# Out-projections of three mixers: the first weight units multiplied with tokens 0 to 127 ahead of the rest

## What is computed

```python
x = x + even_mixer(h, ...)     # ends in  concat(attention, delta rule) @ even_w_out
...
x = x + odd_mixer(h, ...)      # ends in  attention @ odd_w_out
...
m = gate_a * y_a + gate_b * y_b + gate_c * y_c
x = x + m @ w_out
```

## Time and profile before

| what | value |
|---|---|
| median of 3 runs | 1814.69 us (1814.22 to 1814.96) |
| profiled execution | 1815.65 us |
| its span, first to last instruction | 1813.9 us |
| TensorE busy with products (PE) | 1720.6 us, 95% |
| VectorE, ScalarE busy | 1296.1 us (71%), 992.0 us (55%) |
| mean granted TensorE clock | 0.976 |

### The profile page before, as it was taken

One profiled execution on the slowest core, in us unless ns is written; L12 is line 12 of the kernel. 1 busy time (PEld: TensorE's weight loads), 2 busy tenths in 40 slices (PEclk: granted clock), 3 DMA queues, 4 the chain that ended last, 5 costly groups with the idle time before them and its releaser, 6 DMA issues.

```text
span 1813.9 us, 38431 instructions
## 1 busy us (share of the span) xinstructions
PE 1720.6 (95%) x14850; PEld 1609.8 (89%) x14850; DVE 1296.1 (71%) x2130; ACT 992.0 (55%) x1543; POOL 2.5 (0%) x8
## 2 busy tenths in 40 slices
PE   6999899989999999998989999989999998789998
PEld 5999899888999989998988999989999997689997
DVE  5777766657777887777757777877787773557776
ACT  5444554445444564445445444568878874344443
POOL 0000000000000000000000000000000000000000
PEclk9999989999999999999999999999999999899999
DMA  5555443215555455554415555545555540135553
GB/s 206 187 185 184 140 139 108 68 34 169 176 191 186 157 168 178 189 183 137 150 61 167 183 187 185 161 157 182 177 181 178 176 139 4 61 125 178 184 182 120
DMA packets 75577, 277.74 MB, mean 153 GB/s; under 512 B 8400, under 2 KB 8528, under 8 KB 74960
## 3 DMA queue, kind: packets, MB, share of 16 engines
q1 hardware_dynamic: 75024, 273.58, 46.1%
q0 software_dynamic: 448, 2.62, 0.4%
HBM read 274.07 MB, written 2.10 MB: 152 GB/s over the span
## 4 chain that ended last, share of the span: by engine, by line
PE 88%; DVE 6%; ACT 4%; issue 1%; DMA 0%; SPq 0%; DVEq 0%; ACTq 0%
PE ps L458 86%; DVE w_lo L447 1%; PE ps L2211 1%; ACT h L513 1%; ACT w_hi L439 1%; DMA par<-parameters 0%; DVE rstd L541 0%; DVE arena L605 0%; DVE rstd L595 0%; DVE h L534 0%; DVE arena L728 0%; DVE x L758 0%; DVE arena L732 0%; ACT arena L1879 0%; ACT arena L518 0%
## 5 line engine op out<-in xcount | busy, mean ns | idle before, releaser
L458 PE MATMUL ps<-h,w_hi 128*128 128x256 f32 (+1 forms) x4468 | 1101.8, 327 | 0.0
L458 PE MATMUL ps<-h,w_lo 128*128 128x256 f32 x3026 | 868.3, 288 | 44.4 <-DVE w_lo L447 17.7
L458 PEld LDWEIGHTS ps<-h,w_hi 128*128 128x128 f32 x4468 | 761.6, 194 | 68.4
L447 DVE TENSOR_TENSOR w_lo<-raw,w_hi 128x1024 fp32r<-128x1024 f32 x514 | 623.1, 1214 | 118.7 <-ACT w_hi L439 109.1
L439 ACT ACTIVATE w_hi<-raw 128x1024 fp32r<-128x1024 f32 x514 | 538.7, 1050 | 256.0 <-PE ps L458 244.1
L458 PEld LDWEIGHTS ps<-h,w_lo 128*128 128x128 f32 x3026 | 585.1, 193 | 53.5 <-issue 41.3
L458 PE MATMUL ps<-a_hi,w_lo 128*128 128x256 f32 x1032 | 294.2, 285 | 9.3 <-DVE a_lo L748 9.3
L458 PE MATMUL ps<-a_hi,w_hi 128*128 128x256 f32 x1032 | 293.1, 284 | 0.0
L458 PE MATMUL ps<-a_lo,w_hi 128*128 128x256 f32 x1032 | 292.9, 284 | 0.0
L713 ACT ACTIVATE arena<-ps 128x256 f32<-128x256 f32 x208 | 79.4, 384 | 278.6 <-PE ps L458 278.6
L458 PEld LDWEIGHTS ps<-a_hi,w_lo 128*128 128x128 f32 x1032 | 197.5, 191 | 11.2 <-DVE a_lo L748 10.9
(11 more groups left out here) (319 smaller groups left out, 1043.1 us busy)
## 6 DMA issues: line engine op xcount, KB each, us to landing
raw<-weights SPq DMA_DIRECT2D x514, 512.0 KB, 3.3
con<-shape_constants SPq DMA_DIRECT2D x1, 1750.0 KB, 8.6
x<-x_t SPq DMA_DIRECT2D x1, 1024.0 KB, 4.9
stored<-x POOLq DMA_DIRECT2D x1, 1024.0 KB, 5.1
x<-stored POOLq DMA_DIRECT2D x1, 1024.0 KB, 5.2
out_t<-arena SPq DMA_DIRECT2D x4, 256.0 KB, 2.1
arena<-p_t POOLq DMA_DIRECT2D x2, 256.0 KB, 3.6
par<-parameters SPq DMA_DIRECT2D x1, 172.5 KB, 8.6
```

Of the source, the lines that this page charges most:

```text
L447: V.tensor_tensor(w_lo[:, u % RING, 0:n], raw[:, u % RING, 0:n], f(w_hi[:, u % RING, 0:n]), SUB)\
L458: return TE.matmul(o, lhsT, rhs, start=start, stop=stop, skip_group_check=True)
```

## The change

A unit may be multiplied in two parts. `out_first` multiplies unit m with tokens 0 to 127 (24 products of 128 columns) and signals nothing; `out_later` multiplies the same unit with tokens 128 to 255 and raises `s_prod`. `out_pe` takes a list of units that have had their first part and calls `out_later` for these. The other units are multiplied as before.

- even: units 1 and 2. The first part of unit 1 stands behind `weighted(1, 6)`, that of unit 2 behind `turn_back(1, 4)`; the waits for `ob0` and `pt1_2` are moved up to it.
- odd: units 0, 1 and 2. First parts stand behind `turn(1, 3, 3)`, behind `weighted(1, 1, 7)` and behind `turn_back(1, 1, 1)`.
- second: units 0, 1 and 2. First parts stand between `tb2` and `tb3` (one) and behind `tb3` (two). VectorE's order is changed: `rest_of(0)` and `rest_of(1)` are moved ahead of `scaled(3)` and of `gated(2)`.

```diff
--- before.py
+++ after.py
@@ -816,13 +816,29 @@
                     last.then_inc(s_x, 1)


-        def out_pe(pe, s, u0):
+        def out_first(pe, u0, m):
+
+            pe.wait_ge(s_lo, nth(u0 + m))
+            for k in range(KT):
+                wmm(ps[:, 4 + m % 3, 0:P], u0 + m, k, h_hi[:, k, 0:P], h_lo[:, k, 0:P], k == 0, k == KT - 1)
+
+        def out_later(pe, u0, m):
+
+            pe.wait_ge(s_lo, nth(u0 + m))
+            for k in range(KT):
+                last = wmm(ps[:, 4 + m % 3, P:T], u0 + m, k, h_hi[:, k, P:T], h_lo[:, k, P:T], k == 0, k == KT - 1)
+            last.then_inc(s_prod, 1)
+
+        def out_pe(pe, s, u0, split):
             for m in range(KT):
                 if m >= 3 and m % 2:
                     pe.wait_ge(s_add, 4 * n_lin[s] + (m - 3) // 2 + 1)
                 elif m >= 3:
                     pe.wait_ge(s_x, 4 * order[s] + (m - 3) // 2 + 1)
-                linear(pe, u0 + m, ps[:, 4 + m % 3, 0:T])
+                if m in split:
+                    out_later(pe, u0, m)
+                else:
+                    linear(pe, u0 + m, ps[:, 4 + m % 3, 0:T])

         def out_act(act, u0):
             act_split(act, u0 + KT + 1)
@@ -1244,12 +1260,15 @@
                 turn(1, 3, 7)
                 output_spread()
                 weighted(1, 6)
+                va("ob0")
+                sa("pt1_2")
+                out_first(pe, u0 + 27, 1)
                 sa("pt1_1")
                 turn_back(1, 4)
+                out_first(pe, u0 + 27, 2)
                 va("out1")
-                va("ob0")
                 va("ob1")
-                out_pe(pe, "even", u0 + 27)
+                out_pe(pe, "even", u0 + 27, (1, 2))

             def act_prog(act):
                 did = lambda ins, n: ins.then_inc(scalar_done, scalar.step(n))
@@ -1814,13 +1833,17 @@
                 turn(1, 2, 2)
                 weighted(1, 0, 6)
                 turn(1, 3, 3)
+                va("out0_0")
+                va("out0_1")
+                out_first(pe, u0 + 17, 0)
                 turn_back(1, 0, 0)
                 weighted(1, 1, 7)
+                out_first(pe, u0 + 17, 1)
                 turn_back(1, 1, 1)
-                for qb in range(NB):
-                    for b in range(2):
-                        va(f"out{qb}_{b}")
-                out_pe(pe, "odd", u0 + 17)
+                out_first(pe, u0 + 17, 2)
+                va("out1_0")
+                va("out1_1")
+                out_pe(pe, "odd", u0 + 17, (0, 1, 2))

             def act_prog(act):
                 did = lambda ins, n: ins.then_inc(scalar_done, scalar.step(n))
@@ -2086,7 +2109,7 @@
                                       "hh0 sq3 hh1 sd3 hh2 hh3").split())
             adder = Steps(p_vector, ("m0_0 t0_0 tile7 m1_0 m0_1 t0_1 t1_0 m2_0 t2_0 m1_1 t1_1 m3_0 t3_0 mk0 m2_1 t2_1 "
                                      "m4_0 t4_0 m3_1 mk1 t3_1 m5_0 mr0 t5_0 m4_1 t4_1 m5_1 mk2 t5_1 s0 mr1 mk3 va0 s1 yn0 "
-                                     "va1 s2 yn1 va2 M0 yn2 M1 M2 va3 h0 yn3 h1 M3 h2 m").split())
+                                     "va1 s2 yn1 va2 M0 yn2 M1 h0 va3 h1 yn3 M2 M3 h2 m").split())
             small = 7

             def nth_unit(t, n):
@@ -2446,11 +2469,17 @@
                 va("M0")
                 va("yn2")
                 did(turned(yt, 2, 6), "tb2")
+                va("h0")
+                va("h1")
+                out_first(pe, u0 + 98, 0)
                 va("M1")
                 va("yn3")
                 did(turned(yt, 3, 7), "tb3")
+                out_first(pe, u0 + 98, 1)
+                va("M2")
+                out_first(pe, u0 + 98, 2)
                 va("m")
-                out_pe(pe, "second", u0 + 98)
+                out_pe(pe, "second", u0 + 98, (0, 1, 2))

             names = ("ca ga gtb sa sw aa p1 p2 p3 nk cx ya u t1 lw cum cl r k kr k2 tmp "
                      "gb si g2 ea th mu gc bp").split()
@@ -2992,11 +3021,11 @@
                 gated(0)
                 scaled(2)
                 gated(1)
+                rest_of(0)
+                summed(3)
+                rest_of(1)
+                scaled(3)
                 gated(2)
-                summed(3)
-                rest_of(0)
-                scaled(3)
-                rest_of(1)
                 gated(3)
                 rest_of(2)
                 rest_of(3)
```

## The result

The changed kernel takes 1832.82 us (median of 10 runs, 1819.21 to 1838.29) beside 1815.29 us (1814.22 to 1820.06) for the kernel before. The ratio is 1.0084 with a 95% interval of 1.0068 to 1.0101: it is slower by 12 to 18 us, where +3.4 was forecast. The times fall apart: two of the ten are 1819.21 and 1820.86, with a mean granted clock of 0.982 and 0.980, the other eight lie between 1829.3 and 1838.3, with 0.970 to 0.975. The profiled execution, 1834.17 us, is of the larger group.

The account below looks back on a forecast made before the run. The prediction took TensorE, busy for 95% of the span, to bound the kernel. Even +0.7, odd +3.1 and second -0.4 gave +3.4 us on the median 1814.69, so 1818.1 us, range 1806 to 1823.

Parts of the forecast that it names:

- The price of a short product: All three mixers: a 128-column fp32r product is bound by its stationary load, 0.112 us against 0.120 for 256 columns.
- Rival 1: Short products aren't bound by the load: at the skill's 81 ns, -8.5 us, 1806.2 us; chance 0.12.
- rival 2: Short fp32r products fall back to plain float32 pace, 0.223 us each: 1860.7 us; chance 0.10.
- Even +0.7 and odd +3.1: Out-projections: even starts 2.6 us later, runs 2.0 shorter; odd starts 3.8 later, runs 0.65 shorter, no cold stretch to win.
- Second, the first short product: Second block: `h1` is there at about 1576.1, and TensorE starts the first part at 1576.26 after one load.
- Second, from there on: Second block: out-projection starts 2.4 us later and takes 22.63 instead of 25.47, the low clock gone; sum -0.4 us.
- Rival 3: Load binds, but low clock stays or moves: one or two cold stretches on top, 1819.5 to 1821.6 us; chance 0.14.
- What was hidden stayed hidden: All three mixers: VectorE's steps end behind TensorE's added work, so TensorE doesn't wait for them after the first parts.

Follow-up runs that it names:

- e6_filled_second: Against the kernel before, only the second block changed, with 12 unused 256-column products filling TensorE's idle time ahead of `h0` and `h1`: 1815.78 us, ratio 0.9996.
- the cut in place: Against the kernel before, second block only: three units cut into short products, all first parts behind the wait for `m`: 1836.88 us, ratio 1.0114.

## Why the prediction was wrong, step by step

- **The price of a short product: right.** Taken as 0.112 from loads ahead of one- and 64-column products. The loads of the first short ones in the kernel after:

```profile
390.46 0.19 PEld L458 LDWEIGHTS ps<-h,w_lo 128*128 128x128 f32 x1
390.58 0.30 PEld L458 LDWEIGHTS ps<-h,w_hi 128*128 128x128 f32 x2
390.80 0.19 PEld L458 LDWEIGHTS ps<-h,w_lo 128*128 128x128 f32 x1
390.91 0.30 PEld L458 LDWEIGHTS ps<-h,w_hi 128*128 128x128 f32 x2
391.13 0.19 PEld L458 LDWEIGHTS ps<-h,w_lo 128*128 128x128 f32 x1
```

  Three products take 0.335 us (390.46, 390.80, 391.13), 0.112 each. That the columns don't set the pace at the full clock is shown by the wide run too: twice the columns in each of the short ones, and 28.78 us for 240 products, 0.120 each, only 7% more. That it is the load is what is left, with the load rows of the prediction behind it. Rival 1 with 0.081 falls, and the 81 ns of the Trainium skill (page "TensorE: Matmul & The Clock Gate", section "Back-to-back issue gap") don't hold for these four-byte operands; rival 2 with 0.223 falls as well.
- **Even +0.7 and odd +3.1: right for the traces compared**, +0.68 and +3.02. The out-projection of even ran at 1.00 from its start, as assumed. That there is no cold stretch to win in odd was read from one execution; six of ten traces with odd uncut have one, so beside the median odd costs less.
- **Second, the first short product: right.** The working had the first short product at 1576.26, 2.20 us after the transposes of `tb2` began at 1574.06. In the kernel after these begin at 1578.43, and the product follows 2.15 us later. First the transposes before, then both after:

```profile
1574.06 0.66 PE L2211 MATMUL ps<-con,arena 128*128 128x128 f32 x4
```

```profile
1578.43 0.66 PE L2234 MATMUL ps<-con,arena 128*128 128x128 f32 x4
...
1580.58 0.30 PE L458 MATMUL ps<-h,w_lo 128*128 128x128 f32 x1 [1.49 <-DVE h L2978]
```

- **Second, from there on: the step that failed.** The prediction said "Duration 22.63 instead of 25.47, the low clock gone: 2.8 shorter", and it took the first parts at 0.112 as well ("two first parts to 1584.77", a start 2.4 later). The clock wasn't gone. 1.49 us of idle time were left ahead of `h1`, and in the traced execution, and by the times in eight of ten, the clock fell behind them. Some 130 short products then went at 0.213 instead of 0.112. The out-projection began at 1595.3, behind the landmark 8.6 us later than before instead of 2.4, and took 30.9 us instead of 22.63: 6.2 and 8.3 us, the whole miss of 14.5. With the idle time filled the same 240 products took 27.80 us, where the working had 28.0.
- **Rival 3 named the mechanism and had its size wrong.** It priced a cold stretch "as the ones shown", 15 or 23 products. Those were shown with whole products behind them, which end a cold stretch themselves. Short ones of fp32r don't: the stretch is as long as their series, here 30.7 us. The term was 130 x 0.1 = 13 us for the short products and 1 us more for the first whole ones, not the 1.4 to 3.5 us that one or two stretches of the shown size make. The 1832.82 us measured are beyond its 1819.5 to 1821.6 as well. The same text had noted that no row shows the clock in a series of short products, and then priced it by rows of other products.
- **What was hidden stayed hidden.** Nowhere after the first parts did TensorE wait for `out1`, `out1_1` or `m`; the chain goes straight on in TensorE in all three mixers, and in the second block also at the full clock (27.80 us without a break in `e6_filled_second`).

The Trainium skill, page "TensorE: Matmul & The Clock Gate", section "Why this matters for your kernels", advises to keep TensorE continuously busy to get to the full clock. These runs limit that: busy in the profile isn't enough. TensorE shows as busy for 30.57 of the 30.60 us of the cut in place, and the clock stays at 0.50.

## What to carry to other kernels

Cutting a product's moving side saves next to nothing once the load of the stationary matrix sets the pace (0.112 against 0.120), so work put ahead costs its full price outside the idle time: 5.4 us of TensorE for a unit that took 2.9. Before work is placed behind a wait, look not only at the clock now but at whether the new series can raise it again, since a series that can't makes a short cold start as long as itself. Where idle time ahead of a dense stretch costs the clock, filling it with full-width products of no use gave more than the early real work did: 3.9 us under before, some 1 us of it from VectorE's order, where the whole change with its idle time filled was 4.5 over. And one trace shows one execution: a cold stretch that it lacks may be there in most others.

## What the runs showed of the hardware

- A gapless series of 144 fp32r products of 128 columns, 30.6 us long, left the granted clock at 0.50; the same series with 256 columns had it at 1.00 after 5.1 us. At 1.00 the short series held it, for 16.5 us. Plain float32 instructions of 128 columns brought it back within 3.5 us.
- The clock fell 0.8 and 1.5 us into short products that followed 1.49 us of idle time; in one trace of the same code it didn't fall.
- A stationary matrix of 128 x 128 four-byte numbers takes 0.11 us to load at the full clock in fp32r as in float32, so fp32r products of 128 columns go at 0.112 and of 256 at 0.120.
- The low clock shows the two lengths the same: 0.2125 for 128 columns and 0.213 to 0.219 (5.04 us for 23) for 256.
